# Hybrid encoder layer: border keys of the dilated mixer read with their neighbours, in runs of 160 columns

## Chip, cores and metric

The kernel runs on one core of a Trainium2 chip, in one launch. The metric is the device time in microseconds (us) of that execution. Before the change it is 3554.98 us, the median of three runs (3549.92 to 3555.53).

## The reference, cut to what matters

The layer takes 2048 tokens of width 1024. One normalised input goes through a combined projection into the queries, keys and values of two mixers of eight heads of 64 channels each; their outputs are normalised, projected and added to the input. A squared-ReLU MLP of width 4096 and a gated product with a second input follow. The change touches the second mixer:

```python
DILATED_PATTERNS = ((128, 1), (512, 4), (2048, 16))
# one pattern: queries and keys of one residue modulo `dilation`,
# |key - query| <= window / 2, T5 bias by distance, softmax; then the three
# patterns are merged with their denominators
sc = einsum('brnqhd,brnkhd->brnqhk', qs, ks) * HEAD_DIM ** -0.5
sc = where(valid, sc + bias, NEG_BIG)
e = exp(sc - max(sc));  den = sum(e);  o = einsum(e, vs) / den
```

Since the merge weighs each pattern by its own denominator, a key counts once for each pattern that reaches it. The kernel puts that count into the bias table, as a logarithm, and so needs one softmax for each query.

## The kernel before, in words

The program has four stages, one after the other: the projection (to 448 us of the span), the first mixer (to 1238 us), the second mixer (1238 to 1688 us, `mixer_b_phase`), and a feed stage for the output projection, the MLP and the gate. Products are made in a 32-bit matmul format with values split in a high and a low part.

**Tiles of the second mixer.** Tokens are stored by their residue modulo 4, 512 tokens each (`RES`, `SUB`), and a query block is 128 tokens of one residue r: block n has r = n // 4 and b = n % 4, so a head has 16 blocks. Its keys are:
- `own`: up to four 128-key tiles of its own residue (three where b is 0 or 3);
- `oth`: the 128 keys at the same place b in each of the three other residues;
- `ends`: the 16 keys before and the 16 behind that place, in all four residues: 128 columns.

The scores of a block fill two PSUM banks (1024 columns): own in the first, oth and ends in the second. Each part is a pair of matmuls with the query tile as weights: high keys, then low keys. Since the own residue is left out of oth, the three others are one run of 384 columns where r is 0 or 3, and a run of 128 and one of 256 where r is 1 or 2. So a block takes 6 or 8 score matmuls (L1261, L1268, L1274).

**The loop.** All engines go through head after head, 16 blocks a head, with a `Fori` over four pairs of heads. In step n, with N = 16 h + n:
- TensorE: `scores(N+2)`, in steps 2 to 9 also `prepare`, four transposes (L1246) for the next head's queries and keys; then `turn(N+1)` (transposes the exponentials, L1284, after `exp_done`), `fold_out` (L1306) and `values(N)` (L1298);
- VectorE: `add_bias(N+2)` (L1420: three fused add-and-maximum instructions, from PSUM and a bias table into `prob`, and L1423), `output` (L1442), `turned_lo(N+1)` (L1430);
- ScalarE: in steps 2 to 9 `pre_out` (L1349), `turned_hi` (L1365), `exponential(N+2)` (L1358), `sums_out` (L1371);
- GpSimd (POOL): `split_pre` for each prepared tile, `summed` for each pair of blocks (L1206, L1211), and after the eighth tile, in one sequence: `summed` of pair 3, `split_values` (L1196, L1198: the next head's values into high and low part), `summed` of pair 4, `tables` (L1162 to L1171: bias tables of the next head copied into the layout that VectorE reads), `summed` of pairs 5 and 6.

`add_bias` of step 14 is the first that reads the next head's tables and waits for all copies (`t_done_pool`). `output` waits for the `summed` that frees its buffer (`y_ready`); `summed` waits for the store of the staging half that it writes (`y_out`).

**The queue of transfers.** SyncE (SP) issues all of them in a fixed order: for each head two stores of output (L1103), queries and keys of the next head (L90), its values (L96, and eight small ones for the borders, L103), two stores, and two table loads (L109, L115). At the end of the last head it loads constants and two pairs of split weights for the feed stage (L143) and the first rows of the mixers' outputs (L146, L147). The feed stage begins with four loads of the layer's input (L1633) and two further weight pairs (L1620).

Of the kernel before, what the change touches and what calls it, by code (L numbers as in the profile page):

```python
# [20 lines left out]
P = 128  # L21
# [47 lines left out]
class HeadInputs:  # L69
# [3 lines left out]
    VT = NU + RES  # L73
    QK_DMAS, V_DMAS = 4, 1 + 2 * RES
# [19 lines left out]
    def load_v(self, sp, h):  # L94
        v_in, vB = self.v_in, self.scr["vB"]
        sp.dma_start(v_in[:, 0:self.NU, :], vB[PAD:PAD + S, bass.ds(h * HD, HD)].rearrange(  # L96
            "(j p) c -> p j c", p=P)).then_inc(self.v_dma, 16)

        for r in range(RES):
            for side in range(2):  # L100
                row = r * SUB + side * (P + PAD)
                a = vB[row:row + PAD, bass.ds(h * HD, HD)]
                sp.dma_start(v_in[(2 * r + side) * PAD:(2 * r + side + 1) * PAD, self.NU:self.VT, :],  # L103
                             bass.AP(a.tensor, a.offset, [[D_AB, PAD], [P * D_AB, RES], [1, HD]])
                             ).then_inc(self.v_dma, 16)
# [13 lines left out]
class FeedInputs:  # L119
# [6 lines left out]
    def __init__(self, nc, ctx):  # L126
        k = Kit(nc, ctx, "feed")
        self.total = k.sb("total", [P, TT, D], side="right")
        self.w_first = [k.sb(f"w_split{i}", [P, 2, self.CW], F32R, side="right") for i in range(2)]
# [10 lines left out]

    def load_w(self, sp, chunks):
        for C, chunk in enumerate(chunks):
            sp.dma_start(self.w_first[C][:].bitcast(F32), chunk).then_inc(self.w_dma[C], 16)  # L143
# [408 lines left out]
def mixer_a_phase(nc, scr, step, ident, heads, w_ff2, w_late):  # L552
# [11 lines left out]
    with ExitStack() as ctx:  # L564
# [11 lines left out]
        q_raw = k.sb("q_raw", [P, G * P])  # L576
# [142 lines left out]
        def _(pool):  # L719

            pool.memset(pT[0][:, 2:4, :].bitcast(F32), 0.0).then_inc(set_done, 1)
            pool.memset(pT[1][:, 2:4, :].bitcast(F32), 0.0).then_inc(set_done, 1)
            pool.memset(factor[:], 0.0).then_inc(set_done, 1)
# [32 lines left out]
            def query_split(V, g):  # L756
# [3 lines left out]
                pool.tensor_scalar(qT[g][:].rearrange("p h n -> p (h n)"), q_raw[:], 1.0, 0.0, ALU.mult, ALU.add  # L760
# [153 lines left out]
        def _(act):  # L914
# [4 lines left out]
            def query_out(V, bank):  # L919
                act.wait_ge(qt_done, V + 1)  # L920
                act.wait_ge(qt_lo, V * 2 - 2)
                act.activation(q_raw[:], bank[:], ACT.Copy).then_inc(qt_raw, 1)
# [105 lines left out]
def mixer_b_phase(nc, scr, step, ident, heads, feed, consts, chunks):  # L1028
# [9 lines left out]
    VT = NU + RES  # L1038
    SW = S + 2 * PAD
    SLOTS = 4  # L1040
    with ExitStack() as ctx:
# [6 lines left out]
        t_end = [k.sb(f"t_end{u}", [P, 3, RES, RES, 2, PAD]) for u in range(2)]  # L1048
# [29 lines left out]
        T_COPIES = 2 + 3 * RES  # L1078
# [8 lines left out]
        def _(sp):  # L1087
# [33 lines left out]
            feed.load_w(sp, chunks)  # L1121
# [10 lines left out]
            for C in range(2):  # L1132
                sp.wait_ge(feed.w_dma[C], 16)
# [7 lines left out]
        def _(pool):  # L1141
# [16 lines left out]
            def tables(par):  # L1158

                near = t_near[:].rearrange("p (v n) -> p v n", v=7)  # L1160
                for i, v in enumerate((0, 4)):
                    pool.tensor_copy(t_oth[par][:, 3 * i:3 * i + 3, :], near[:, v:v + 3, PAD:PAD + P]  # L1162
                                     ).then_inc(t_done_pool, 1)
                for r in range(RES):
                    a = near[:, 3 - r:7 - r, 0:PAD]
                    both = bass.AP(a.tensor, a.offset, [[TABLE_W - OWN_W, P], [P + 2 * PAD, RES], [P + PAD, 2],
                                                        [1, PAD]])
                    pool.tensor_copy(t_end[par][:, 1, r, :, :, :], both).then_inc(t_done_pool, 1)
                    pool.tensor_copy(t_end[par][:, 0, r, :, 1, :], near[:, 3 - r:7 - r, PAD + P:2 * PAD + P]
                                     ).then_inc(t_done_pool, 1)  # L1170
                    pool.tensor_copy(t_end[par][:, 2, r, :, 0, :], near[:, 3 - r:7 - r, 0:PAD]  # L1171
                                     ).then_inc(t_done_pool, 1)
# [63 lines left out]
        def _(pe):  # L1236
# [13 lines left out]
            def scores(N, par, n):  # L1250
# [12 lines left out]
                at = BANK  # L1263
                runs = [x for x in ((0, r), (r + 1, RES)) if x[1] > x[0]]
                for a, z in runs:
                    for part in range(2):
                        main = kT[par][part][:, PAD:PAD + S].rearrange("p (r m) -> p r m", r=RES)
# [20 lines left out]
            def values(N, h, par, n):  # L1288
# [3 lines left out]
                         [NU + b])  # L1292
# [98 lines left out]
        def _(ve):  # L1391
# [16 lines left out]
            def add_bias(N, par, n):  # L1408
# [5 lines left out]
                parts = ((c0 * P, BANK, t_own[par][:, (3 - b + own) * P:(7 - b + own - c0) * P]),  # L1414
                         (BANK, BANK + 3 * P, t_oth[par][:, 3 - r:6 - r, :].rearrange("p a n -> p (a n)")),
                         (BANK + 3 * P, 2 * BANK, t_end[par][:, edge, r, :, :, :].rearrange("p a s n -> p (a s n)")))
                ve.wait_ge(sc_done, N + 1)
                ve.sem_inc(step, 1)
                for i, (a, z, table) in enumerate(parts):
                    ve.tensor_tensor_reduce(prob[:, slot, a:z], sc[:, a:z], table, 1.0, -3.0e38, ALU.add, ALU.max,  # L1420
# [52 lines left out]
def feed_phase(nc, x, w_ff2, w_tail, pT_d, scr, out, step, ident, feed):  # L1473
# [43 lines left out]
    with ExitStack() as ctx:  # L1517
# [12 lines left out]
        w_sp = feed.w_first + [k.sb(f"w_split{i}", [P, 2, CW], F32R) for i in range(2, NSPL4)]  # L1530
# [55 lines left out]
        def _(sp):  # L1586
# [705 lines left out]
```

## Time and profile before

| what | us |
|---|---|
| median of 3 runs | 3554.98 |
| the profiled execution, own time | 3553.58 |
| its span | 3551.8 |
| TensorE busy in the span | 3411.9 |
| VectorE busy | 2359.8 |
| ScalarE busy | 1882.8 |
| GpSimd busy | 1834.9 |

The span runs from the first to the last instruction of one execution. Busy shares are means over four different stages and don't tell what limits one of them. The mean granted clock of TensorE was 0.982 of full speed. Instructions of TensorE overlap, so what one of them costs is read from the step between starts, not from its duration.

### The profile page before, as it was taken

How to read it: one execution, taken by the hardware profiler on the slowest of the kernel's cores; microseconds unless marked ns; L12 is line 12 of the kernel's file. 1: busy time of each engine (PE TensorE's matmuls, PEld its weight loads, DVE VectorE, ACT ScalarE, POOL GpSimd, SP SyncE). 2: the span in 40 equal slices, each digit the busy share in tenths (PEclk: the TensorE clock that was granted, in tenths of full speed). 3: DMA queues.
4: the chain of work that ended last, by engine and by line, in shares of the span. 5: the costliest groups of instructions: out<-in, count | busy, mean ns of one | idle time of the engine just before them, and what ended most of it. 6: DMA issues, size and time to landing. Idle time of an engine off the chain costs nothing.

```text
span 3551.8 us, 55707 instructions
## 1 busy us (share of the span) xinstructions
PE 3411.9 (96%) x17910; PEld 2869.5 (81%) x17910; DVE 2359.8 (66%) x4254; ACT 1882.8 (53%) x3554; POOL 1834.9 (52%) x1308
## 2 busy tenths in 40 slices
PE   8999979999999999999699999999999999999997
PEld 6878868888888789999578888788887888878885
DVE  5555579999889889899355565555655556555553
ACT  3222268888888777777343354443544435443342
POOL 5555424444552255656157750677606776067760
PEclk9999999999999999999799999999999999999998
DMA  5445434445442144244334447444474444744443
GB/s 182 167 166 179 134 115 147 145 151 181 143 140 77 26 93 85 67 96 114 138 104 146 154 154 259 140 149 152 150 257 148 147 152 144 256 155 142 141 147 111
DMA packets 294318, 510.97 MB, mean 144 GB/s; under 512 B 175988, under 2 KB 194876, under 8 KB 276572
## 3 DMA queue, kind: packets, MB, share of 16 engines
q1 hardware_dynamic: 284764, 494.54, 43.4%
q10 hardware_dynamic: 9344, 13.73, 1.1%
q8 instruction: 119, 1.95, 0.2%
q14 instruction: 91, 0.75, 0.1%
HBM read 425.07 MB, written 95.58 MB: 147 GB/s over the span
## 4 chain that ended last, share of the span: by engine, by line
PE 47%; DVE 2%; ACT 2%; issue 1%; POOL 0%; DMA 0%; SPq 0%; DVEq 0%; ACTq 0%
PE feed_bank L1742 46%; PE feed_bank L1733 1%; ACT feed_xT L1901 1%; POOL feed_w_split L1698 0%; DVE feed_xT L2032 0%; DMA feed_y_in<-scr_yB 0%; DVE feed_total L2047 0%; DVE feed_sums L2153 0%; DVE feed_total L2107 0%; ACT feed_junk L1892 0%; ACT feed_w_split L1928 0%; DVE feed_ms L2011 0%; DVE feed_res L2050 0%; DVE feed_xn L2023 0%; DVE feed_comb L2032 0%
## 5 line engine op out<-in xcount | busy, mean ns | idle before, releaser
L1698 POOL TENSOR_TENSOR feed_w_split<-feed_w_raw,feed_w_split 128x1024 fp32r<-128x1024 f32 x352 | 882.3, 2518 | 258.6 <-ACT feed_w_split L1928 246.7
L1742 PE MATMUL feed_bank<-feed_w_split,feed_comb 128*128 128x512 f32 x3648 | 857.7, 395 | 15.7 <-DVE feed_sums L2153 7.5
L1742 PEld LDWEIGHTS feed_bank<-feed_w_split,feed_comb 128*128 128x128 f32 x3648 | 683.9, 188 | 177.6 <-DVE feed_sums L2153 10.1
L1742 PE MATMUL feed_bank<-feed_xT,feed_w_split 128*128 128x512 f32 x3072 | 712.2, 393 | 2.5 <-DVE feed_xT L2032 2.5
L1742 PEld LDWEIGHTS feed_bank<-feed_xT,feed_w_split 128*128 128x128 f32 x3072 | 578.1, 188 | 134.3 <-DVE feed_xT L2032 2.9
L358 PE MATMUL proj_bank<-proj_w_split,proj_xT 128*128 128x512 f32 (+1 forms) x1920 | 402.8, 370 | 2.4 <-issue 2.4
L1010 DVE TENSOR_TENSOR mixa_pT<-mixa_turned,mixa_pT 128x512 fp32r<-128x512 f32 x512 | 351.3, 686 | 62.0 <-ACT mixa_pT L956 53.0
L1695 POOL TENSOR_SCALAR feed_w_split<-feed_w_raw 128x1024 fp32r<-128x1024 f32 x128 | 135.4, 1058 | 494.6 <-PE feed_bank L1742 292.3
L358 PEld LDWEIGHTS proj_bank<-proj_w_split,proj_xT 128*128 128x128 f32 x1920 | 333.5, 189 | 66.6 <-issue 5.4
L956 ACT ACTIVATE mixa_pT<-mixa_turned 128x512 fp32r<-128x512 f32 x512 | 307.1, 600 | 125.7 <-PE mixa_turned L894 106.5
L853 PE MATMUL mixa_out_acc<-mixa_pT,mixa_v_hl 128*128 128x512 f32 x1028 | 365.5, 437 | 0.7 <-DVE mixa_pT L1010 0.7
L1943 ACT ACTIVATE feed_rl<-feed_bank 128x512 f32<-128x512 f32 x128 | 76.6, 598 | 536.8 <-PE feed_bank L1742 532.9
L2107 DVE TENSOR_TENSOR feed_total<-feed_total,feed_bank 128x512 f32<-128x512 f32 x352 | 224.5, 683 | 202.8 <-PE feed_bank L1742 199.1
L1928 ACT ACTIVATE feed_w_split<-feed_w_raw 128x1024 fp32r<-128x1024 f32 x224 | 236.0, 1062 | 194.3 <-PE feed_bank L1742 189.6
L981 DVE TENSOR_REDUCE mixa_nmax<-mixa_score 128x1 f32<-128x1024 f32 x264 | 322.3, 1222 | 13.2 <-PE mixa_score L840 6.5
L894 PE MATMUL mixa_turned<-layer_ident,mixa_prob 128*128 128x128 f32 x2048 | 307.2, 272 | 0.0
L894 PEld LDWEIGHTS mixa_turned<-layer_ident,mixa_prob 128*128 128x128 f32 x2048 | 252.7, 141 | 55.5
L928 ACT ACTIVATE mixa_prob<-mixa_score,mixa_nmax 128x1024 f32<-128x1024 f32 x263 | 293.9, 1118 | 3.9 <-DVE mixa_nmax L981 3.9
L840 PE MATMUL mixa_score<-mixa_kT,mixa_qT 128*128 128x512 f32 x1056 | 287.9, 394 | 6.9 <-ACT mixa_prob L928 6.2
L2076 DVE TENSOR_TENSOR feed_comb<-feed_rl,feed_comb 128x256 fp32r<-128x256 f32 x128 | 152.4, 1191 | 181.0 <-ACT feed_comb L1947 181.0
L840 PEld LDWEIGHTS mixa_score<-mixa_kT,mixa_qT 128*128 128x128 f32 x1056 | 198.2, 188 | 55.8 <-ACT mixa_prob L928 8.7
L1742 PE MATMUL feed_bank<-feed_w_split,feed_xT 128*128 128x512 f32 x768 | 182.9, 398 | 2.5 <-DVE feed_xT L2032 2.5
(202 smaller groups left out, 5055.6 us busy)
## 6 DMA issues: line engine op xcount, KB each, us to landing
feed_w_raw<-scr_wT SPq DMA_DIRECT2D x160, 512.0 KB, 3.3
feed_w_split<-scr_wG SPq DMA_DIRECT2D x72, 1024.0 KB, 4.9
feed_w_raw<-w_tail_dram SPq DMA_DIRECT2D x128, 512.0 KB, 3.5
proj_w_raw<-w_in_dram SPq DMA_DIRECT2D x39, 1024.0 KB, 5.2
feed_w_raw<-w_ff_dram SPq DMA_DIRECT2D x64, 512.0 KB, 3.4
scr_table<-scr_bias SPq DMA_DIRECT2D x8, 1520.0 KB, 8.4
proj_x_t<-x_dram SPq DMA_DIRECT2D x20, 512.0 KB, 5.7
mixa_q_in<-scr_qA SPq DMA_DIRECT2D x36, 256.0 KB, 3.5
```

The source lines that it names most:

```text
L358: mm = pe.matmul(acc[t][:, 0:width], xT[u][a][:, k0 + kk, t * P:(t + 1) * P], w[m][:, kk, :], start=first and kk == 0 and q == 0, stop=las ...
L840: mm = pe.matmul(score[:, at * BANK:(at + 1) * BANK], qT[g][:, h, :], kT[g][part][:, kc * BANK:(kc + 1) * BANK], start=part == 0, stop=par ...
L853: mm = pe.matmul(out_acc[half][:], v_hl[:, s, g, :], pT[part][:, s % NR, :], start=s % (NT // 2) == 0 and part == 0, stop=s % (NT // 2) == ...
L894: mm = pe.transpose(turned[s % 2][:, h * P:(h + 1) * P], prob[w][:, h, s * P:(s + 1) * P], ident[:])
L928: act.activation(prob[par][:, h, half * 2 * BANK:(half + 1) * 2 * BANK], score[:, 2 * (c % 2) * BANK:2 * (c % 2 + 1) * BANK], ACT.Exp, bia ...
L956: act.activation(pT[0][:, s % NR, :], turned[s % 2][:], ACT.Copy).then_inc(hi_done, 1)
L981: ve.tensor_reduce(nmax[:, par, c // G, c % G:c % G + 1], score[:, 2 * (c % 2) * BANK: 2 * (c % 2 + 1) * BANK], AXX, ALU.max, negate=True) ...
L1010: ve.tensor_tensor(pT[1][:, s % NR, :], turned[s % 2][:], pT[0][:, s % NR, :].bitcast(F32), ALU.subtract).then_inc(lo_done, 1)
L1698: pool.tensor_tensor(w_sp[slot][:, 1, :], w_raw[:, slot, :], w_sp[slot][:, 0, :].bitcast(F32), ALU.subtract).then_inc(w_lo, 1)
L1742: mm = pe.matmul(dst, lhs, rhs, start=start, stop=stop)
L1928: act.activation(w_sp[slot][:, 0, :], w_raw[:, slot, :], ACT.Copy).then_inc(w_hi_ff, 1)
L2107: ve.tensor_tensor(at, at, acc[2 * (n % 2) + t][:], ALU.add if sign > 0 else ALU.subtract).then_inc(ev_dve, 1)
```

## The change

- The 16 border keys on either side are read together with the 128 keys between them: each run of other residues is now (number of residues) x 160 columns, at column 16 of the second bank. The border keys of the own residue are no longer computed. A block has 4 or 6 score matmuls.
- VectorE reads the scores of oth as three pieces of 128 in steps of 160 columns, and those of the borders as four pieces of 32 in steps of 160 (the first and last 16 of them are outside the runs and get a very negative bias). It writes them to the same places in `prob` as before.
- The tile of border values belongs to one residue of the query, since the own residue is left out and the order differs: 16 such tiles a head in place of 4, filled by 24 small transfers in place of 8; the splitting of values goes over 32 tiles in place of 20.
- The tables of the borders are filled by 18 copies in place of 12.
- Memory for this: a staging tile of the first mixer now lies in a bias table of the second, and two weight pairs are loaded at the start of the feed stage (before its loads of the input) and no longer in the second mixer. The first mixer clears the unused rows of the value tiles once.

```diff
-    VT = NU + RES
-    QK_DMAS, V_DMAS = 4, 1 + 2 * RES
+    VT = NU + RES * RES
+    QK_DMAS, V_DMAS = 4, 1 + 2 * RES * (RES - 1)
...
         for r in range(RES):
-            for side in range(2):
-                row = r * SUB + side * (P + PAD)
...
+            for place, x in enumerate([x for x in range(RES) if x != r]):
+                for side in range(2):
+                    row = x * SUB + side * (P + PAD)
+                    a = vB[row:row + PAD, bass.ds(h * HD, HD)]
+                    sp.dma_start(v_in[(2 * place + side + 1) * PAD:(2 * place + side + 2) * PAD,
+                                      self.NU + RES * r:self.NU + RES * (r + 1), :],
...
# mixer_a_phase
-        q_raw = k.sb("q_raw", [P, G * P])
+        q_raw = heads.t_own[1][:, 0:G * P]
+            pool.memset(heads.v_in[:, heads.NU:, :], 0.0)
...
# mixer_b_phase, SP
-            feed.load_w(sp, chunks)
...
# tables
                 for r in range(RES):
-                    a = near[:, 3 - r:7 - r, 0:PAD]
...
+                    for x, z in ((0, r), (r + 1, RES)):
+                        if x == z:
+                            continue
+                        v, to = 3 - r + x, x - (x > r)
+                        pool.tensor_copy(sided(1, r)[:, to:to + z - x, :, :], both).then_inc(t_done_pool, 1)
+                        pool.tensor_copy(sided(0, r)[:, to:to + z - x, 1, :], near[:, v:v + z - x, PAD + P:WIDE]
+                                         ).then_inc(t_done_pool, 1)
+                        pool.tensor_copy(sided(2, r)[:, to:to + z - x, 0, :], a).then_inc(t_done_pool, 1)
...
# scores
-                at = BANK
+                at = BANK + PAD
                 runs = [x for x in ((0, r), (r + 1, RES)) if x[1] > x[0]]
                 for a, z in runs:
                     for part in range(2):
-                        pe.matmul(sc[:, at:at + (z - a) * P], q, main[:, a:z, b * P:(b + 1) * P],
-                                  start=part == 0, stop=part == 1)
-                    at += (z - a) * P
-                for part in range(2):
-                    t = kT[par][part][:, b * P:b * P + PAD]
-                    ends = bass.AP(t.tensor, t.offset, [[SW, P], [SUB, RES], [P + PAD, 2], [1, PAD]])
-                    mm = pe.matmul(sc[:, at:at + P], q, ends, start=part == 0, stop=part == 1)
+                        t = kT[par][part][:, a * SUB + b * P:a * SUB + b * P + WIDE]
+                        wide = bass.AP(t.tensor, t.offset, [[SW, P], [SUB, z - a], [1, WIDE]])
+                        mm = pe.matmul(sc[:, at:at + (z - a) * WIDE], q, wide, start=part == 0, stop=part == 1)
+                    at += (z - a) * WIDE
...
# add_bias
+                wide = sc[:, BANK + PAD:2 * BANK - PAD].rearrange("p (x n) -> p x n", n=WIDE)
+                ends = bass.AP(e.tensor, e.offset, [[2 * BANK, P], [WIDE, RES], [1, 2 * PAD]])
+                         (prob[:, slot, at_oth:at_end].rearrange("p (x n) -> p x n", n=P), wide[:, :, PAD:PAD + P],
+                          t_oth[par][:, 3 - r:6 - r, :]),
+                         (prob[:, slot, at_end:].rearrange("p (x n) -> p x n", n=2 * PAD), ends,
+                          t_end[par][:, edge, r, :].rearrange("p (x n) -> p x n", n=2 * PAD)))
...
# feed_phase, SP
-            for t in range(TT):
-                sp.dma_start(res[:, t, :], x[t * P:(t + 1) * P, :]).then_inc(x_dma[t], 16)
-            for C in range(len(feed.w_first), NG1):
+            for C in range(NG1):
+                if C == NSPL4:
+                    for t in range(TT):
+                        sp.dma_start(res[:, t, :], x[t * P:(t + 1) * P, :]).then_inc(x_dma[t], 16)
                 load_split(C, C, C % NSPL4)
```

## Rows read from the trace of the kernel before

**Rows 1.** The page, part 1: busy us (share) xinstructions.

```profile
PE 3411.9 (96%) x17910; PEld 2869.5 (81%) x17910; DVE 2359.8 (66%) x4254; ACT 1882.8 (53%) x3554; POOL 1834.9 (52%) x1308
```

**Rows 2.** Windows, one head: length, then busy us of PE, PEld, DVE, ACT, POOL; clock.

```profile
1304.00:1358.00 54.00, 53.53 (x431) 51.84 (x429) 50.45 (x177) 44.34 (x92) 32.94 (x49) 1.00 0.46 90
```

**Rows 3.** Waits in the second mixer: us in total, times, longest.

```profile
DVE mixb_prob L1420 <- PE mixb_score L1274: 32.0, 62, 3.6
```

**Rows 4.** Waits of one head, 1302 to 1356 us.

```profile
DVE mixb_prob L1420 <- PE mixb_score L1274: 2.5, 7, 0.6
```

**Rows 5.** Timeline, blocks with `prepare`: start us, us, engine, line, xcount [idle before].

```profile
1380.65 0.62 PE L1268 MATMUL mixb_score<-mixb_kT,mixb_qT 128*128 128x128 f32 x4
...
1381.11 0.34 PE L1274 MATMUL mixb_score<-mixb_kT,mixb_qT 128*128 128x128 f32 x2
...
1381.28 0.62 PE L1246 MATMUL mixb_out_acc<-layer_ident,mixb_q_in 128*128 128x128 f32 x4
...
1385.13 0.56 DVE L1420 CUSTOM_DVE_ANT_0 mixb_prob<-mixb_score,mixb_t_own 128x384 f32<-128x384 f32 x1 [0.34 <-PE mixb_score L1274]
```

**Rows 6.** Timeline, a block without `prepare`.

```profile
1406.65 1.27 DVE L1430 TENSOR_TENSOR mixb_pT<-mixb_turned,mixb_pT 128x512 fp32r<-128x512 f32 x2
...
1407.02 0.51 PE L1268 MATMUL mixb_score<-mixb_kT,mixb_qT 128*128 128x384 f32 x2
...
1407.37 0.33 PE L1274 MATMUL mixb_score<-mixb_kT,mixb_qT 128*128 128x128 f32 x2
...
1407.89 0.56 DVE L1420 CUSTOM_DVE_ANT_0 mixb_prob<-mixb_score,mixb_t_own 128x384 f32<-128x384 f32 x1
```

**Rows 7.** Timeline of POOL: values split, a sum, tables copied, a sum.

```profile
1399.75 1.27 POOL L1196 TENSOR_SCALAR mixb_v_hl<-mixb_v_in 128x1280 fp32r<-128x1280 f32 x1
1401.11 2.95 POOL L1198 TENSOR_TENSOR mixb_v_hl<-mixb_v_in,mixb_v_hl 128x1280 fp32r<-128x1280 f32 x1
1404.01 0.74 POOL L1206 TENSOR_TENSOR mixb_y_part<-mixb_y_part 128x256 f32<-128x256 f32 x1
...
1405.40 0.96 POOL L1162 COPY mixb_t_oth<-mixb_t_near 128x384 f32<-128x384 f32 x2
1406.30 0.30 POOL L1168 COPY mixb_t_end<-mixb_t_near 128x128 f32<-128x128 f32 x1
1406.54 0.24 POOL L1169 COPY mixb_t_end<-mixb_t_near 128x64 f32<-128x64 f32 x1
1406.72 0.24 POOL L1171 COPY mixb_t_end<-mixb_t_near 128x64 f32<-128x64 f32 x1
...
1408.50 0.24 POOL L1171 COPY mixb_t_end<-mixb_t_near 128x64 f32<-128x64 f32 x1
```

**Rows 8.** Groups by line: a POOL subtraction of 1024 columns: busy us, mean ns.

```profile
L803 POOL TENSOR_TENSOR mixb_k_in<-mixb_t_near,mixb_k_in 128x1024 fp32r<-128x1024 f32 x9 | 21.6, 2402 | 1.7 <-POOL mixb_k_in L799 1.7
```

**Rows 9.** Timeline of DVE: `add_bias` of step 14, the head of rows 7.

```profile
1411.05 0.56 DVE L1420 CUSTOM_DVE_ANT_0 mixb_prob<-mixb_score,mixb_t_own 128x384 f32<-128x384 f32 x1
```

**Rows 10.** Timeline: SP's border loads, and POOL's first staging write after them.

```profile
1410.24 2.25 SPq L103 DMA_DIRECT2D mixb_v_in<-scr_vB  x1
...
1412.68 1.33 SPq L103 DMA_DIRECT2D mixb_v_in<-scr_vB  x3
...
1431.38 0.46 POOL L1211 TENSOR_TENSOR mixb_y_st<-mixb_y_part 128x128 f32<-128x128 f32 x1 [0.26 <-ACT mixb_pre L1349]
```

**Rows 11.** Timeline: the first head's values, VectorE and what waited for it.

```profile
1252.03 1.49 DVE L1405 TENSOR_TENSOR mixb_v_hl<-mixb_v_in,mixb_v_hl 128x1280 fp32r<-128x1280 f32 x1 [0.52 <-ACT mixb_v_hl L1353]
...
1253.58 1.76 PE L1284 MATMUL mixb_turned<-layer_ident,mixb_prob 128*128 128x128 f32 x7 [3.84 <-DVE mixb_v_hl L1405]
```

**Rows 12.** POOL's first wait in the first mixer (timeline).

```profile
487.69 0.20 POOL L736 TENSOR_TENSOR mixa_below<-mixa_nrow,mixa_nmax 128x8 f32<-128x8 f32 x1 [36.22 <-DVE mixa_nrow L1016]
```

**Rows 13.** Feed stage, first products (timeline) and transfers (windows; DMA share and GB/s last).

```profile
1708.65 26.73 PE L1742 MATMUL feed_bank<-feed_w_split,feed_xT 128*128 128x512 f32 x105 [2.46 <-DVE feed_xT L2032]
...
1698.00:1702.00 4.00, 2.13 (x10) 1.43 (x8) 3.45 (x13) 3.56 (x15) 0.00 (x0) 0.50 0.64 270
1702.00:1706.00 4.00, 2.13 (x10) 1.43 (x8) 2.87 (x10) 2.60 (x11) 0.00 (x0) 0.50 0.00 0
```

**Rows 14.** The bias addition of oth (groups by line: busy us, mean ns).

```profile
L1420 DVE CUSTOM_DVE_ANT_0 mixb_prob<-mixb_score,mixb_t_oth 128x384 f32<-128x384 f32 x130 | 71.9, 553 | 0.0
```

More of the change, by code:

```diff
@@ L99, in load_v @@
         for r in range(RES):
-            for side in range(2):
-                row = r * SUB + side * (P + PAD)
[L102 to L105, printed above, removed]
+            for place, x in enumerate([x for x in range(RES) if x != r]):
[4 more added lines that the diff above has]
+                                      self.NU + RES * r:self.NU + RES * (r + 1), :],
+                                 bass.AP(a.tensor, a.offset, [[D_AB, PAD], [P * D_AB, RES], [1, HD]])
+                                 ).then_inc(self.v_dma, 16)
     def load_near(self, sp, h):
@@ L128, in __init__ @@
         self.total = k.sb("total", [P, TT, D], side="right")
-        self.w_first = [k.sb(f"w_split{i}", [P, 2, self.CW], F32R, side="right") for i in range(2)]
         self.g_row = k.sb("g_row", [P, 2, D], side="right")
@@ L1025, in _, with mixer_b_phase @@
             output(4 * NT + 1, 1, 1)
-def mixer_b_phase(nc, scr, step, ident, heads, feed, consts, chunks):
+def mixer_b_phase(nc, scr, step, ident, heads, feed, consts):
     NU = 16
     NK = 8
-    VT = NU + RES
+    VT = heads.VT
+    WIDE = P + 2 * PAD
     SW = S + 2 * PAD
@@ L1047, in mixer_b_phase @@
         t_oth = [k.sb(f"t_oth{u}", [P, 6, P]) for u in range(2)]
-        t_end = [k.sb(f"t_end{u}", [P, 3, RES, RES, 2, PAD]) for u in range(2)]
+        t_end = [k.sb(f"t_end{u}", [P, 3, RES, P]) for u in range(2)]
         prob = k.sb("prob", [P, SLOTS, 2 * BANK])
@@ L1131, in _ @@
             sp.wait_ge(feed.const_in, feed.CONSTS)
-            for C in range(2):
-                sp.wait_ge(feed.w_dma[C], 16)
             for s in feed.out_dma:
@@ L1163, in tables @@
                                      ).then_inc(t_done_pool, 1)
+                sided = lambda e, r: t_end[par][:, e, r, PAD:P - PAD].rearrange("p (x s n) -> p x s n", s=2, n=PAD)
                 for r in range(RES):
[L1165 to L1172 removed]
+                    for x, z in ((0, r), (r + 1, RES)):
+                        if x == z:
+                            continue
+                        v, to = 3 - r + x, x - (x > r)
+                        a = near[:, v:v + z - x, 0:PAD]
+                        both = bass.AP(a.tensor, a.offset, [[TABLE_W - OWN_W, P], [WIDE, z - x], [P + PAD, 2], [1, PAD]])
+                        pool.tensor_copy(sided(1, r)[:, to:to + z - x, :, :], both).then_inc(t_done_pool, 1)
+                        pool.tensor_copy(sided(0, r)[:, to:to + z - x, 1, :], near[:, v:v + z - x, PAD + P:WIDE]
+                                         ).then_inc(t_done_pool, 1)
+                        pool.tensor_copy(sided(2, r)[:, to:to + z - x, 0, :], a).then_inc(t_done_pool, 1)
             pool.wait_ge(set_done, 9)
@@ L1529, in feed_phase @@
         w_raw = k.sb("w_raw", [P, NR4, CW])
-        w_sp = feed.w_first + [k.sb(f"w_split{i}", [P, 2, CW], F32R) for i in range(2, NSPL4)]
+        w_sp = [k.sb(f"w_split{i}", [P, 2, CW], F32R) for i in range(NSPL4)]
         res = k.sb("res", [P, TT, D])
@@ L2269, in layer @@
             mixer_b_phase(nc, scr, step, ident, heads, feed,
-                          ((g_out, g_mlp_pre, g_ple), (g_attn_post, g_mlp_post)),
-                          [scr["wG"][C] for C in range(2)])
+                          ((g_out, g_mlp_pre, g_ple), (g_attn_post, g_mlp_post)))
         feed_phase(nc, x, w_ff2, w_tail, pT, scr, out, step, ident, feed)
```

23 lines of the change are left out of this document (10 added, 13 removed).

## The prediction

> **What bounds the kernel now.** The page comes first: TensorE is busy for nearly the whole span, VectorE for two thirds of it [rows 1]. That mean hides the stage that is changed, so I took windows next. In a head of the second mixer TensorE is busy for 53.53 of 54.00 us and VectorE for 50.45 [rows 2]: the two are almost level, and a saving on the one is worth only what the other leaves. The waits tell how they share the time. VectorE waited for scores 62 times, 32.0 us in all [rows 3]; in one head it was 2.5 us in 7 waits [rows 4]. The timeline shows where. In the blocks of steps 2 to 9, in which TensorE also makes four transposes for the next head, VectorE stands still before its first bias addition [rows 5]. In a block without them VectorE's subtractions begin at 1406.65, their pair takes 1.27, and the next bias addition starts at 1407.89: nothing between, while the scores for it were made at 1407.37 [rows 6]. So each head has eight blocks bound by TensorE and eight bound by VectorE.
>
> **Score matmuls.** Removed are two matmuls of 128 columns a block; the rest grow from 128, 256 or 384 columns to 160, 320 or 480. All blocks with `prepare` compute scores of residues 1 and 2 (step n makes block n+2, that is 4 to 11), which had six matmuls outside the own keys. They ran from 1380.65 to 1381.28, 0.63 us, or 0.105 us each whether they had 128 or 256 columns [rows 5]; matmuls of 384 stand (1407.37 - 1407.02) / 2 = 0.175 apart [rows 6]. A matmul of 160 lies inside the flat part: 0.105. One of 320 lies halfway between 256 and 384: 0.14. Four of them take 0.49 and save 0.14; if 320 costs as much as 384, 0.56 and 0.07; if as much as 256, 0.42 and 0.21. I take 0.13, a little less for the steps in which VectorE already leaves nothing. 64 such blocks: 8.3 us saved, between 4.5 and 13.4. VectorE's idle time in one head, 2.5 us or 20 in all eight [rows 4], would allow each of these, so it is not next to bind there. The 64 blocks without `prepare` give nothing: what is freed on TensorE is covered by VectorE, which has no gap [rows 6].
>
> **Bias additions.** Count and elements of VectorE's three instructions stay; two of them read in pieces. The trace has no reading of PSUM in pieces of 32. From below a piece costs nothing (I see no reason for a gain); from above I double the instruction of oth, +0.55 us a block [rows 14]. I take nothing, since the addresses only step at another stride and the elements come in the same number; the upper end is a rival below.
> The Trainium skill, "SBUF — State Buffer", section "Door 1: The DMA port swizzle", says that PSUM is reached in lines of two fp32 values and that non-contiguous access to it slows matmuls significantly. Here every piece is contiguous for at least 32 values and starts on an even column, so the rule itself would charge only the jumps; by it the sum might stay, and a reader who applies it to the whole instruction gets the second rival. No row of this trace decides it.
>
> **The splitting of values.** POOL splits 32 tiles of 64 columns, 2048, in place of 1280. The subtraction took 2.95 at 1280 columns [rows 7] and 2.40 at 1024 [rows 8]: 2.15 ns a column, so 768 more cost 1.65. The conversion took 1.27 [rows 7]; its share of the growth is at most 0.6 x 1.27 = 0.76, and I take 0.65. Together 2.3 us a head later for all that stands behind it on POOL.
>
> **The copies.** A copy of 128 columns has its successor 0.24 us behind (1406.54 - 1406.30), one of 64 columns 0.18 (1406.72 - 1406.54) [rows 7]: 0.12 us and 0.94 ns a column. Before: 12 copies with 1024 columns, 2.4 us. After: 18 with 768, 18 x 0.12 + 0.72 = 2.9. Another 0.5 us.
> These two were hidden by POOL's idle time; now they meet a wait. The last copy ended at 1408.50 + 0.24 = 1408.74 [rows 7]. With 2.3 and 0.5 it is 1411.5. VectorE begins the additions of step 14 at 1411.05 [rows 9], and they wait for all copies. So the cover of 2.3 us is gone and 0.5 us of stall is left, in every head. Behind that instruction stand VectorE's output and subtractions of the step, for which TensorE waits in `values`, so it goes straight to the end: 8 x 0.5 = 4.0 us. If the copies are a little quicker, or if TensorE reaches the eighth `prepare` earlier against VectorE, it is 0; if short copies hold 0.24 each, 6 x 0.12 more, 1.2 us a head and 10 in all. The sum of the pair at 1404.01 moves to 1406.3 and is done 1.5 later; it frees a buffer that VectorE writes after the additions begun at 1407.89, so there is no second stall [rows 6, 7].
>
> **SP and the border loads.** 16 more transfers a head. In the head shown, the first of the eight is held for 2.4 us by the large load before it; then three take 1.33, less than 0.51 from start to start, as the ring has room [rows 10]. 16 x 0.5 = 8 us later for what is queued behind them: two stores and two table loads. The stores free the staging half that POOL writes at 1431.38 [rows 10]. The loads ended near 1416 (1412.68 and seven steps of 0.5); now it is 1424. There are 7 us left for the store to land; the cost is nothing.
> By the Trainium skill, "DMA: Bandwidth & Descriptors", section "Bandwidth", transfers below 64 KB are governed by their descriptors; these have 16 KB. That speaks against the change. In this trace it shows as issue time on SP, not as a wait of an engine, and the sum is the same with it and without.
>
> **Start and end of the stage.** The first head's values are split by ScalarE and VectorE, and TensorE waited 3.84 us for that [rows 11]. VectorE's 1.49 grows by 0.6 to 2.3 at most, I take 0.8; ScalarE's conversion before it grows by about the same 0.6. +1.4 us, once. The clearing in the first mixer is of 1024 columns and stands where POOL then idles for 36.22 us: nothing [rows 12]. The feed stage loads 4 MB before its first product, as before (two pairs and the input; now four pairs). They all had landed by 1702, and the first product was at 1708.65, released by VectorE [rows 13]. The input follows the pairs, some 8 us later, long before its first use after the first products. Nothing; should it be late, every microsecond beyond these 6.6 would count in full.
>
> **Sum.** -8.3 + 4.0 + 1.4 = -2.9 us. The profiled execution took 3553.58, so it would take 3550.7. That execution lies 1.4 us below the median of the runs shown, inside their spread; I give 3550.5.
>
> **Rivals.**
> (1) POOL is just in time, or TensorE's saving is at its upper end. For it: the stall is a difference of two numbers of over ten microseconds. Against it: all terms come from measured steps. Without the stall 3553.58 - 8.3 + 1.4 = 3546.7; with 13.4 saved besides, 3541.6.
> (2) The reads in pieces are slower: slower than before. Its place is the two additions on VectorE; x us a block fall in full on the 64 blocks bound by VectorE, and above 0.15 also on the others, where VectorE has 0.3 idle. The saving of 2.9 is eaten at x = 0.045, and at 0.16 the kernel is 7 us slower. At the upper end, 0.55, 64 x 0.55 + 64 x 0.4 gives 61 us: 3612. At 0.2 it is 3567. The page on SBUF of the Trainium skill, named above, has the rule that would bring it about.
> (3) SP becomes the bound: if each of the 16 loads takes over 1 us, stores land after 1431.38, POOL stands in `summed`, and VectorE waits for it: 1 to 2 us a head, 3559 to 3567. Against it: the steps of 0.5 in rows 10.
> (4) The change doesn't do what it says: a matmul of 320 or 480 costs its columns over again, and nothing is saved. Then 3553.58 + 5.4 = 3559.
>
> **How the numbers follow.** Forecast 0.48, (1) 0.30, (2) 0.08, (3) 0.07, (4) 0.07. A measurement of this kernel tells about 0.2%, 7.1 us, from no change. Beyond it on the fast side lies most of (1) and a little of the forecast: 0.31. On the slow side most of (2), half of (3), little of (4), and a copy stall of 10: 0.17. The rest, 0.52, is no change. The range leaves out the far ends of (1) and (2): 3540 to 3562; that of the forecast alone is 3546 to 3556.
>
> **What would show it.** Right: the step between the first matmul outside the own keys and the first of `prepare` at 0.5 us; VectorE's waits for scores down from 2.5 us a head to about 1.5; a new wait of VectorE's L1420 for POOL's copies, once a head, near 0.5 us; the addition of oth at 553 ns as before; the first product of the feed stage as far behind the stage's start as now. Wrong: additions that take longer, waits of POOL for stores, or a block without `prepare` that gets shorter, which would mean that VectorE was not what bound it.

## The result, and the profile after

The changed kernel takes 3531.76 us (median of 4 runs, 3527.85 to 3533.06) against 3553.89 of the kernel before on the same chip (3549.92 to 3555.53): 0.9938 of its time, 95% interval 0.992 to 0.9955. I had forecast 3550.5 and a range from 3540. The profiled execution's span went from 3551.8 to 3529.3 us. All of it came from a place where I had written "Nothing".

The page, part 1, of the changed kernel (busy us, share, instructions) has 37.4 us less of TensorE than [rows 1], 22 more of POOL, and of VectorE and ScalarE what they had:

```profile
PE 3374.5 (96%) x17650; PEld 2838.6 (80%) x17650; DVE 2362.2 (67%) x4254; ACT 1886.9 (53%) x3554; POOL 1856.9 (53%) x1363
```

The first product of the feed stage (timeline: start us, us, engine, line, tiles, count, idle before) stands at 1708.97, against 1708.65 in [rows 13]. So the two mixers together saved nothing, and 22.8 us of 1843 came after that point:

```profile
1708.97 3.36 PE L1745 MATMUL feed_bank<-feed_w_split,feed_xT 128*128 128x512 f32 x7 [2.46 <-DVE feed_xT L2035]
```

**The feed stage.** Its matmuls are the same ones in the same order: 7488 of 512 columns. Each chunk of weights serves 24 or 12 of them and lies in one of four pairs of tiles (`w_split0` to `w_split3`) that take turns. The query by tile (duration in ns: least, median, most) shows only a median that fell from 395 and 393 ns, and a matmul's recorded duration is not its step. First the kernel before, then after:

```profile
L1742 PE MATMUL feed_bank<-feed_w_split,feed_comb x3648: 387/395/794, 1833.1 to 3546.6; 128*128 128x512 f32 x192
L1742 PE MATMUL feed_bank<-feed_xT,feed_w_split x3072: 389/393/796, 1786.0 to 3422.8; 128*128 128x512 f32 x192
```

```profile
L1745 PE MATMUL feed_bank<-feed_w_split,feed_comb x3648: 387/389/793, 1831.6 to 3524.2; 128*128 128x512 f32 x192
L1745 PE MATMUL feed_bank<-feed_xT,feed_w_split x3072: 387/389/795, 1785.1 to 3401.4; 128*128 128x512 f32 x192
```

The timeline of four chunks in a row says where the loss was. Each line is cut so that it starts with a chunk: x25 is its 24 matmuls and the first of the next, and the starts of two lines lie 24 steps apart. The operand named first is the one that is moved through TensorE. The kernel before:

```profile
1732.89 5.99 PE L1742 MATMUL feed_bank<-feed_w_split,feed_xT 128*128 128x512 f32 x25
1738.48 6.00 PE L1742 MATMUL feed_bank<-feed_w_split,feed_xT 128*128 128x512 f32 x25
1744.08 5.86 PE L1742 MATMUL feed_bank<-feed_w_split,feed_xT 128*128 128x512 f32 x25
1749.55 5.83 PE L1742 MATMUL feed_bank<-feed_w_split,feed_xT 128*128 128x512 f32 x25
```

and after:

```profile
1732.32 5.83 PE L1745 MATMUL feed_bank<-feed_w_split,feed_xT 128*128 128x512 f32 x25
1737.76 5.83 PE L1745 MATMUL feed_bank<-feed_w_split,feed_xT 128*128 128x512 f32 x25
1743.20 5.83 PE L1745 MATMUL feed_bank<-feed_w_split,feed_xT 128*128 128x512 f32 x25
```

Before, the chunks in pairs 0 and 1 took 5.59 and 5.60 us, 233.2 ns a matmul; those in pairs 2 and 3 took 226.7 to 228. After, each chunk takes 5.44 us, 226.7. Over the stage the steps of pairs 0 and 1 were 233.25 ns on average and are 226.7 to 227.2. Windows of 470 us in the middle of the stage (columns as in [rows 2]), first before, then after, hold 20 instructions of TensorE more:

```profile
2160.00:2630.00 470.00, 466.55 (x2081) 380.34 (x2080) 264.86 (x438) 205.39 (x383) 253.83 (x120) 1.00 0.53 179
```

```profile
2160.00:2630.00 470.00, 465.79 (x2101) 384.81 (x2101) 268.88 (x443) 210.69 (x391) 253.90 (x120) 1.00 0.53 180
```

Half of 7488 matmuls times 6.3 ns (233.25 less some 226.9) is 24 us, which is the gain of the whole kernel and 1 more. Against it stands a wait of TensorE for POOL's splitting of weights, which grew by 4.2 us (us, times; first before, then after):

```profile
  POOL feed_w_split L1698: 1.9, 6
```

```profile
  POOL feed_w_split L1701: 6.1, 16
```

Pairs 0 and 1 are the ones that the change moved. Before, they were allocated at the upper end of SBUF, where `load_w` could fill them while the second mixer still ran. The allocation puts them at bytes 204768 and 196576 of each partition; the changed kernel has all four side by side from 138240 on. `xT` and `comb` did not move (31744, 48128, 64512).

**The second mixer.** Of the changed kernel: a window of one head (as [rows 2]), waits of the stage (as [rows 3]), TensorE and VectorE around a block with `prepare` (as [rows 5]), the addition of `oth` (as [rows 14]).

```profile
1304.00:1358.00 54.00, 52.36 (x402) 48.16 (x399) 50.14 (x177) 44.03 (x91) 36.47 (x59) 1.00 0.47 94
```

```profile
DVE mixb_prob L1422 <- PE mixb_score L1268: 19.2, 46, 4.1
DVE mixb_prob L1422 <- POOL mixb_t_end L1171: 8.3, 8, 1.1
```

```profile
1384.23 0.65 PE L1268 MATMUL mixb_score<-mixb_kT,mixb_qT 128*128 128x320 f32 x4
1384.71 0.61 PE L1245 MATMUL mixb_out_acc<-layer_ident,mixb_k_in 128*128 128x128 f32 x4
...
1385.07 0.56 DVE L1422 CUSTOM_DVE_ANT_0 mixb_prob<-mixb_score,mixb_t_own 128x384 f32<-128x384 f32 x1 [0.18 <-PE mixb_score L1268]
```

```profile
L1422 DVE CUSTOM_DVE_ANT_0 mixb_prob<-mixb_score,mixb_t_oth 128x384 f32<-128x384 f32 x130 | 71.9, 553 | 0.0
```

The score matmuls outside the own keys take 0.48 us where they took 0.63; VectorE waits 12.8 us less for scores. But a new line has 8.3 us in 8 waits for POOL's copies, once a head. The timeline of that place, which answers to [rows 7, 9]:

```profile
1399.18 1.91 POOL L1195 TENSOR_SCALAR mixb_v_hl<-mixb_v_in 128x2048 fp32r<-128x2048 f32 x1
...
1401.17 4.61 POOL L1197 TENSOR_TENSOR mixb_v_hl<-mixb_v_in,mixb_v_hl 128x2048 fp32r<-128x2048 f32 x1
...
1407.13 0.95 POOL L1158 COPY mixb_t_oth<-mixb_t_near 128x384 f32<-128x384 f32 x2
...
1410.74 0.23 POOL L1171 COPY mixb_t_end<-mixb_t_near 128x48 f32<-128x48 f32 x1
...
1411.25 0.56 DVE L1422 CUSTOM_DVE_ANT_0 mixb_prob<-mixb_score,mixb_t_own 128x384 f32<-128x384 f32 x1 [1.03 <-POOL mixb_t_end L1171]
```

And the start of the stage, as [rows 11], with ScalarE's conversion ahead of it (the first line is that of before, the second the one after):

```profile
1250.74 1.26 ACT L1353 ACTIVATE mixb_v_hl<-mixb_v_in 128x1280 fp32r<-128x1280 f32 x1
```

```profile
1251.09 1.89 ACT L1348 ACTIVATE mixb_v_hl<-mixb_v_in 128x2048 fp32r<-128x2048 f32 x1
...
1253.02 2.29 DVE L1400 TENSOR_TENSOR mixb_v_hl<-mixb_v_in,mixb_v_hl 128x2048 fp32r<-128x2048 f32 x1 [1.42 <-ACT mixb_v_hl L1348]
...
1255.37 1.76 PE L1279 MATMUL mixb_turned<-layer_ident,mixb_prob 128*128 128x128 f32 x7 [6.20 <-DVE mixb_v_hl L1400]
```

### The profile page after: what moved, and what is told of

Its sections match the earlier page's. It is cut to its first block, busy times and chain, and to the rows that moved or that the text cites. A ratio compares the mean times of both kernels' runs of the same rounds, so it can differ in the third digit from the quotient of the medians.

```text
span 3529.3 us, 55481 instructions
## 1 busy us (share of the span) xinstructions
PE 3374.5 (96%) x17650; PEld 2838.6 (80%) x17650; DVE 2362.2 (67%) x4254; ACT 1886.9 (53%) x3554; POOL 1856.9 (53%) x1363
## 4 chain that ended last, share of the span: by engine, by line
PE 47%; DVE 2%; ACT 2%; issue 1%; POOL 0%; DMA 0%; SPq 0%; DVEq 0%; ACTq 0%
PE feed_bank L1745 46%; PE feed_bank L1736 1%; ACT feed_xT L1904 1%; DVE feed_xT L2035 0%; POOL feed_w_split L1701 0%; DMA feed_y_in<-scr_yB 0%; DVE feed_total L2050 0%; DVE feed_sums L2156 0%; DVE feed_total L2110 0%; ACT feed_junk L1895 0%; ACT feed_w_split L1931 0%; DVE feed_res L2053 0%; DVE feed_ms L2014 0%; DVE feed_xn L2026 0%; DVE feed_comb L2035 0%
## 5 line engine op out<-in xcount | busy, mean ns | idle before, releaser
L1745 PE MATMUL feed_bank<-feed_w_split,feed_comb 128*128 128x512 f32 x3648 | 845.6, 392 | 18.3 <-DVE feed_sums L2156 7.8
L1745 PE MATMUL feed_bank<-feed_xT,feed_w_split 128*128 128x512 f32 x3072 | 702.0, 390 | 2.5 <-DVE feed_xT L2035 2.5
```

The lines of the kernel that those rows point to most:

```text
L1745: mm = pe.matmul(dst, lhs, rhs, start=start, stop=stop)
```

## The experiments

Steps named below are the differences between the starts of neighbouring matmuls of one chunk, averaged over all chunks of a pair that have `xT` as one operand (some 400 to 740 differences each; those with a wait in between are left out).

**The feed stage's part alone.** The kernel before, with only this:

```diff
-        self.w_first = [k.sb(f"w_split{i}", [P, 2, self.CW], F32R, side="right") for i in range(2)]
-        w_sp = feed.w_first + [k.sb(f"w_split{i}", [P, 2, CW], F32R) for i in range(2, NSPL4)]
+        w_sp = [k.sb(f"w_split{i}", [P, 2, CW], F32R) for i in range(NSPL4)]
```

and all four pairs loaded at the start of the feed stage.

> The kernel before with the feed stage's part alone: the two weight pairs live with the other two and are loaded at the stage's start; scores, bias additions, border values and copies as before. Theory P (placement): in the trace of before the step between matmuls is 233.3 ns for the pairs in slots 0 and 1, whose tiles begin 32 bytes behind a multiple of 64, and 226.7 ns for slots 2 and 3; in the changed kernel it is 226.7 for all. 3744 matmuls x 6.6 ns = 24.6 us, so this kernel takes about 24 us less than before (3530 +- 4) and is level with the changed kernel; all four slots at 226.7. Rival S (scores): the gain comes from the fewer score matmuls of the second mixer; then this kernel is level with before (3554).

Measured: 3530.46 us, ratio 0.9934 (0.992 to 0.9947), all steps 226.7 to 227.3 ns. The second mixer in it is that of before, down to VectorE's wait for scores:

```profile
DVE mixb_prob L1412 <- PE mixb_score L1266: 32.2, 62, 3.5
```

So the feed stage's part gives the whole gain, and the second mixer's part gives nothing that the whole time shows.

**Two pairs moved by 32 bytes.** The question now was what about the place counts: the region at the upper end, or the exact byte. The changed kernel, with every pair on the lower side:

```diff
-        w_sp = [k.sb(f"w_split{i}", [P, 2, CW], F32R) for i in range(NSPL4)]
+        shift0 = k.sb("shift0", [P, 8])
+        w_sp = [k.sb(f"w_split{i}", [P, 2, CW], F32R) for i in range(2)]
+        shift1 = k.sb("shift1", [P, 8])
+        w_sp += [k.sb(f"w_split{i}", [P, 2, CW], F32R) for i in range(2, NSPL4)]
```

> The changed kernel with the tiles of weight pairs 0 and 1 moved by 32 bytes (unused columns before and behind them), nothing else. Theory P with alignment as the cause: slots 0 and 1 step 233.3 ns again, slots 2 and 3 stay at 226.7, and the time rises by 24.6 us to about 3556, level with before. Rival R (region): what cost was the place at the upper end of the memory, above 196 KB, not the 32 bytes; then nothing changes (3532). Rival S: nothing changes.

Measured: 3568.0 us, ratio 1.0039 (1.0026 to 1.0053). Two paddings of eight floats cost 36 us. The same four chunks:

```profile
1734.93 5.99 PE L1748 MATMUL feed_bank<-feed_w_split,feed_xT 128*128 128x512 f32 x25
1740.52 6.00 PE L1748 MATMUL feed_bank<-feed_w_split,feed_xT 128*128 128x512 f32 x25
1746.12 5.89 PE L1748 MATMUL feed_bank<-feed_w_split,feed_xT 128*128 128x512 f32 x25
1751.62 5.89 PE L1748 MATMUL feed_bank<-feed_w_split,feed_xT 128*128 128x512 f32 x25
```

The region is not what counts; the byte is. But more was lost than expected. The two paddings add up, so pairs 2 and 3 were moved too, by 64 bytes, against what the expectation says, and they slowed: 229.0 ns where they are moved through TensorE, and 233.3 where they are its weights (`xT` moved). A multiple of 64 is not enough.

**The kernel before, its right side moved down by 32 bytes.** Pairs 0 and 1 then begin at 204736 and 196544, multiples of 64:

```diff
+        self.shift = k.sb("shift", [P, 8], side="right")
         self.w_first = [k.sb(f"w_split{i}", [P, 2, self.CW], F32R, side="right") for i in range(2)]
```

> The kernel before with 32 unused bytes ahead of the two weight pairs at the upper end of the memory, so that they begin at multiples of 64; loads, scores and everything else as before. Theory P with alignment: all slots at 226.7 ns, 24.6 us less than before, about 3530. Rival R (region): slots 0 and 1 stay at 233.3 and the time at 3554. Rival S: 3554.

Measured: 3546.17 us, ratio 0.9977 (0.9968 to 0.9986), a third of the gain. As weights the two pairs take 229.0 ns (before 233.3), moved they still take 233.3. The expectation of 226.7 everywhere failed. Set beside the run before it, this is the mirror image: there +64 bytes cost 6.6 ns as weights and 2.3 moved, here -64 cost 2.3 as weights and 6.6 moved. That suggests that only the difference between the starts of the two operands counts.

**All operands moved by 32 bytes.**

```diff
+        shift0 = k.sb("shift0", [P, 8])
         xT = [k.sb(f"xT{h}", [P, KD, BT], F32R) for h in range(2)]
         ...
+        shift1 = k.sb("shift1", [P, 8])
         res = k.sb("res", [P, TT, D])
```

> The changed kernel with the feed stage's other operands (xT, comb) and all four weight pairs begun 32 bytes later each, so that the pairs stand to their partners exactly as in the changed kernel, and only the absolute place differs. Theory R (what counts is the difference of the start addresses of the two operands of a matmul, the weights' minus the moving one's): difference 0 as in the changed kernel, all steps 226.7 ns, 3532 us. Theory A (each operand by itself must begin on a large unit): every step 233.3 ns or more, over 3555 us, some 3575.

Measured: 3532.09 us, ratio 0.9935 (0.9919 to 0.9952), every step 226.7 to 227.4, in the same four chunks too:

```profile
1739.66 5.83 PE L1747 MATMUL feed_bank<-feed_w_split,feed_xT 128*128 128x512 f32 x25
1745.10 5.83 PE L1747 MATMUL feed_bank<-feed_w_split,feed_xT 128*128 128x512 f32 x25
1750.54 5.83 PE L1747 MATMUL feed_bank<-feed_w_split,feed_xT 128*128 128x512 f32 x25
```

No operand begins on a multiple of 64 here, and nothing is lost. It is the difference, not the place.

**Three ladders.** Since the pairs take turns, one kernel gives the step at four differences:

```diff
-        w_sp = [k.sb(f"w_split{i}", [P, 2, CW], F32R) for i in range(NSPL4)]
+        w_sp = []
+        for i, pad in enumerate((32, 16, 16, 16)):     # e8: (0, 16, 16, 16); e9: (24, 16, 88, 128)
+            if pad:
+                k.sb(f"shift{i}", [P, pad])
+            w_sp.append(k.sb(f"w_split{i}", [P, 2, CW], F32R))
```

The second ladder also has 16 floats ahead of `xT`.

> The changed kernel with xT and comb in place and the four weight pairs moved by 128, 192, 256 and 320 bytes, one look for the steps of each pair (the pairs take turns, so one trace gives four). Rows so far, as difference (weights minus moving) and step: 0: 226.7; +64: 233.3; -64: 229.0; +32 and -32: 233.2. Theory R1 (the unit is 128 bytes): pair 0 and pair 2 at 226.7, pairs 1 and 3 as +64 or -64. Theory R2 (the unit is 256 bytes): only pair 2 at 226.7, and pair 3 as +64 (xT as moving operand 233.3, the others 229.0). Theory R3 (512 bytes): none at 226.7.

> The changed kernel with xT and comb moved by 64 bytes and the four weight pairs by 64, 128, 192 and 256 bytes: differences of 0, 64, 128 and 192 bytes to their partners, from another absolute start. Theory R (difference alone): pair 0 at 226.7; pair 1 at 233.3 where it holds the weights (xT moving) and 229.0 where it moves; pairs 2 and 3 the same steps as pairs 0 and 1 of the run with 128, 192, 256 and 320. Theory A (each operand's own start): pair 0 slow although its difference is 0, and pair 3, which begins on 256 bytes, no slower than pair 0.

> The changed kernel with xT and comb in place and the four weight pairs moved by 96, 160, 512 and 1024 bytes; one look for the steps of each pair. Theory R2 (the difference of the two start addresses counts, in a unit of 256 bytes): pairs 2 and 3 as in the changed kernel, 226.7 to 227.3 ns; pairs 0 and 1 (96 and 160) near 233, since 32, 64 in one direction and 128 gave 232.5 to 233.4. Rival (the unit is larger, and 256 bytes only came near): pairs 2 and 3 differ from 226.7 by 1 ns or more.

One run of each gave 3560.53, 3554.85 and 3560.02 us. Chunks with `xT` moved and the pairs 1, 2 and 3 as weights, in the first ladder (weights begin 192, 256 and 320 bytes behind) and in the second (64, 128, 192 behind):

```profile
1798.42 5.89 PE L1749 MATMUL feed_bank<-feed_xT,feed_w_split 128*128 128x512 f32 x25
1803.92 5.83 PE L1749 MATMUL feed_bank<-feed_xT,feed_w_split 128*128 128x512 f32 x25
1809.37 5.99 PE L1749 MATMUL feed_bank<-feed_xT,feed_w_split 128*128 128x512 f32 x25
```

```profile
1792.69 5.99 PE L1750 MATMUL feed_bank<-feed_xT,feed_w_split 128*128 128x512 f32 x25
1798.28 5.96 PE L1750 MATMUL feed_bank<-feed_xT,feed_w_split 128*128 128x512 f32 x25
1803.85 5.91 PE L1750 MATMUL feed_bank<-feed_xT,feed_w_split 128*128 128x512 f32 x25
```

All runs together, by where the weight pair begins against its partner `xT`, in bytes modulo 256 (-32 and -64 stand at 224 and 192), mean step in ns:

| pair begins behind its partner by | pair as weights, `xT` moved | pair moved, `xT` as weights |
|---|---|---|
| 0 | 226.7 to 228.2 | 226.9 to 227.9 |
| 32 | 233.3 | 233.1 to 233.3 |
| 64 | 233.3 to 233.4 | 229.0 to 229.4 |
| 96 | 234.1 | 233.7 |
| 128 | 232.5 | 232.6 to 232.8 |
| 160 | 233.8 | 234.1 |
| 192 | 229.0 to 229.2 | 233.3 to 233.5 |
| 224 | 233.3 | 233.3 |

Differences of 256, 512 and 1024 bytes fall into the first line (227.3, 228.2 and 226.7 as weights); the unit is 256 bytes, and 128 is not one. The two columns agree once the difference is taken as weights minus moving: 192 costs 2.3 ns in both, every other one 5.8 to 7.4. In the second ladder `xT` begins elsewhere and the values stay. These are means: near 229 the single steps of a chunk are a mix, for example 226, 229 and 232 in turn.

The table leaves out the chunks with `comb` as weights, 3648 matmuls. Their means have the same order: 226.7 to 229.5 at 0, 228.8 to 230.4 at 64, and 232.7 to 234.2 at the other differences. Pairs at difference 0 that take turns with slow ones had up to 1.5 ns more than 226.7 in the table and up to 2.8 with `comb`. The excess lies in the first four to eight matmuls of a chunk that follows a slow one: in the kernel before, pair 2 with `comb` began with steps of 230, 233, 229, 230 and 229 ns and then kept 227. Why a slow chunk reaches into the next is open.

**The short wait.** To the second mixer: in the changed kernel VectorE waits, before the additions of step 14, for all 20 copies, of which those additions need 5. The rest is now waited for before the additions of step 2 of the next head:

```diff
-    ve.wait_ge(t_done_pool, h * T_COPIES + 2 * T_COPIES)
+    ve.wait_ge(t_done_pool, h * T_COPIES + T_COPIES + 5)
     ...
                         if n < NU - 2:
+                            if n == 2:
+                                ve.wait_ge(t_done_pool, h * T_COPIES + T_COPIES)
                             add_bias(N + 2, par, n + 2)
```

> The changed kernel, but VectorE waits in step 14 only for the first 5 of the 20 table copies (those of oth and of residue 0) and for the rest before the additions of step 2 of the next head. Theory: in the changed kernel VectorE waited 8 times for POOL's copies, 8.3 us in all; 15 copies of about 0.15 us stand behind the fifth, 2.2 us, more than the 1.0 us that each wait lasted, so the wait goes and 7 to 8 us with it: about 3524 against 3532 of the changed kernel. Rival: the wait only moves to the next engine in the ring (TensorE waits for the exponentials and VectorE's subtractions in the same place) and less than 3 us come back.

Measured: 3525.16 us, ratio 0.9914 (0.9901 to 0.9928), under the changed kernel's 3531.76. The interval overlaps that of the changed kernel (0.992 to 0.9955), though none of its five runs (up to 3525.75) reaches any of the other's four (from 3527.85); the waits carry the point. The line of POOL's copies is gone, and a part comes back as waits for scores (19.2 before this edit):

```profile
DVE mixb_prob L1422 <- PE mixb_score L1268: 27.0, 52, 4.5
```

From the first to the last bias addition of own keys the second mixer takes 432.5 us in the kernel before, 432.1 changed, and 427.4 with the short wait. Of the 5.9 us by which the profiled span is shorter than the changed kernel's, 3.5 lie ahead of the feed stage's first product (1705.5 against 1708.97). The rest comes behind it, where TensorE's wait for POOL's weights is 1.7 us in place of 6.1. No run shows what moves that wait, so not all of the gain is shown to be that of the edit.

**The rule tried in the mixers.** In the second mixer `kT` has a size of 8320 bytes, so the second half of each key tile begins 128 bytes off. To the kernel with the short wait this adds 32 floats behind each key tile:

```diff
+                kT[u].append(k.sb(f"kT{u}{h}", [P, SW], F32R))
+                k.sb(f"kT_pad{u}{h}", [P, 32])
```

> The kernel with the short wait, and in the second mixer 128 bytes behind each of the four key tiles, so that all four begin on 256 bytes as the query tile does (now the second of each pair is off by 128). With theory R2 the second half's score matmuls outside the own keys go from a step of some 232 to 227 ns for 480 columns, and those of the own keys from 233 to 229 at 512: 2 x 128 x some 5 ns = 1.3 us of TensorE, of which half lies in steps that TensorE bounds: 0.6 us less than the kernel with the short wait (3525.2), 3524.5. If the rule doesn't hold outside the feed stage: 3525.2. Both are within what is told apart in the whole time; the starts of the matmuls in the trace decide. Faster than both kernels by either.

Measured: 3525.72 us, ratio 0.9923 (0.9909 to 0.9936): no gain. The trace speaks against the expectation for the own keys, too. Those of the second half had steps of 229 ns for 512 columns and now have 233 to 234, those of the first stayed at 235. Weights minus moving is now 192 for both, which cost only 2.3 ns in the feed stage.

In the first mixer I put 64 bytes between the key tiles:

```diff
+            if i:
+                k.sb(f"kT_pad{i}", [P, 16])
+            kT[i // 2].append(k.sb(f"kT{i // 2}{i % 2}", [P, S], F32R))
```

> The kernel with the short wait, and in the first mixer the key tiles of each head pair and half moved by 0, 64, 128 and 192 bytes against the query tiles (all four begin on 256 bytes in every kernel so far, and yet the steps of its score matmuls of 512 columns are 228 to 236 ns, 232 on average, not 226.7). One look. If the rule of the feed stage holds on top of something that these matmuls have besides: the steps of the moved three rise, to some 235 to 239 on average. If where the tiles begin plays no part where one set of weights is read again and again: 231 to 232 in all four, 3525. A fall under 229 for one of them would be worth having (1056 matmuls).

Measured: 3523.8 us in one run. The mean steps by place in a block of four went from 232.2, 232.0, 231.3 and 232.3, 232.2, 230.8 to 230.1, 231.8, 233.9 and 233.2, 230.9, 235.3: they moved, both ways, by up to 4.5 ns. So the start matters there as well, but neither of my two theories for it fits. What these matmuls have besides (they use one set of weights several times in a row) wasn't separated.

## Why the prediction was wrong

**The step that failed** is in "Start and end of the stage": the feed stage's loads, "Nothing". I asked only when the four pairs would be loaded. That was right: the first product is 0.3 us later than before, as level as the forecast had it. I didn't ask where the pairs would lie. The edit took two of four from the upper end of SBUF, where they stood 224 bytes modulo 256 behind their partners, to a place with difference 0, and 3744 matmuls became 6.3 ns shorter on average: -24 us, for which the sum had no term and no rival. That the kernel got faster was luck: nothing in the change aimed at where the pairs begin. The profile of before had it: the starts of the four chunks shown above lie 5.59, 5.60 and 5.47 us apart, for the same 24 matmuls. I had read the stage at its first product alone [rows 13], and a group's mean mixes the four pairs.

The Trainium skill, "Advanced Engine Details and Errata", section "Memory Cachelines", gives SBUF lines of 16 bytes. All tiles here begin on multiples of 32, so that rule alone would have made every one of these placements equal; the runs have 226.7 against 233.3, and the measurement decides.

**Score matmuls**: I had -8.3 us, 4.5 to 13.4. By the starts of VectorE's additions of own keys, the steps 2 to 9 took 27.37 us a head and take 26.17, mean over the heads: -1.20, or -9.6 in eight. Right within its bounds. TensorE's 0.48 us for the two matmuls of 160 and the two of 320 was forecast as 0.49. There two errors offset each other: the starts of single matmuls, averaged over the stage, are 0.094 us apart for 160 columns (forecast 0.105) and 0.156 for 320 (forecast 0.14). The flat part that I read between 128 and 256 columns was a mean over both sizes; before, they stood 0.085 and 0.131 apart.

**Bias additions**: nothing. The addition of `oth`, in pieces of 128, takes 553 ns as before, and that of the borders, in pieces of 32, 287 ns against 286. Rival (2), reads in pieces, falls.

**The splitting of values and the copies**: from the start of the splitting to the end of the copies it was 8.99 us [rows 7] and is 1410.97 - 1399.18 = 11.79: +2.8, as forecast (2.3 and 0.5). Yet the stall is 1.04 us and not 0.5, 8.3 us in all for 4.0. I compared the later copies with VectorE's old time. VectorE would now have been ready at 1411.25 - 1.03 = 1410.22, 0.83 earlier; POOL had started only 0.57 earlier, and 0.28 passes from the end of the last copy to the addition: 0.49 + 0.83 - 0.57 + 0.28 = 1.03. Part of what the score matmuls saved had run into the wait. Without the wait at that place the stage was 4.7 us shorter, not 8.3: VectorE then waits 7.8 us more for scores.

**Start of the stage**: the term of +1.4 was right: ScalarE's conversion grew by 0.63 (1.26 to 1.89), VectorE's subtraction by 0.80 (1.49 to 2.29). TensorE's wait went from 3.84 to 6.20, +2.4, and shows more than that cost, since the conversion started 0.35 later and TensorE was ready 0.57 earlier (1255.37 - 6.20 = 1249.17, before 1253.58 - 3.84 = 1249.74).

**SP**: no wait for a store appeared; rival (3) falls, and rival (4) with the steps above. -9.6 + 8.3 + 1.4 = +0.1 us for the second mixer against my -2.9; from its first addition to its last the trace has -0.4. The kernel with the feed stage's part alone is 1.3 us faster than the whole change. None of these can be told from nothing. The sum isn't complete: steps 0 and 1 took 0.29 us a head more (three heads of seven took 7.3 to 7.9 us for the two, before the change one did, and the others 6.3 to 6.5), and no run shows why.

## What to carry to other kernels

An edit that moves a tile is an edit of every matmul that reads it: work out where both operands begin before and after, and read the steps between matmul starts tile by tile, not a group's mean. In a stage like this one, begin a matmul's two operands at the same byte modulo 256; where the tiles begin was worth 0.7% here, and two paddings of eight floats lost 1%. And where an edit makes an engine earlier, hold its new time, not the old one, against each wait on another engine; wait only for the part of a transfer or a copy that the next instruction reads.

## What the runs showed of the hardware that I had not expected

- fp32r matmuls (the 32-bit format) of 512 columns with new weights each, at granted clock 1.00, with `xT` as one operand: a mean step of 226.7 ns when both operands begin at the same byte modulo 256 (up to 228.2 beside slow chunks), 229.0 to 229.4 when weights minus moving is 192, and 232.5 to 234.1 at the six other differences tried. Only the difference counts: 226.7 with all operands on multiples of 64 and with none. Within a chunk the weights of a matmul and those of the next begin at the same byte modulo 256, so the runs don't tell which of the two meets the operand that is being moved.
- Even the best step is 13.4 ns over 512 columns at 2.4 GHz (213.3). The Trainium skill, "TensorE: Matmul & The Clock Gate", section "Back-to-back issue gap", has 2.5 ns over it for an isolated matmul; no run here came to that.
- In the mixers, where consecutive matmuls share their weights, the steps of 512 columns are 231.8 ns on average in the first and 229 and 235 (second and first key tile) in the second, and answer to the start of the tiles in another way. This stays open, as does the cause inside the chip of the feed stage's rule.
- On POOL a copy of 16 to 96 columns has its successor 0.14 to 0.21 us behind (means over all heads), so what counts is mostly how many copies there are.
